# Way down of the experts: 128-column products in two column halves, or 256-column products in two contraction halves

## What is computed

```python
def expert_block(args):
    xblk, e = args
    hid = jax.nn.silu(xblk @ w_gate[e]) * (xblk @ w_up[e])   # 1024 -> 512
    return hid @ w_down[e]                                   # 512 -> 1024
```

## Time and profile before

| | |
|---|---|
| median of 3 runs | 4352.32 us |
| profiled execution | 4360.02 us, span 4358.2 us |
| TensorE (PE) busy | 3815.1 us, 88% of the span |
| VectorE (DVE) busy | 1654.0 us, 38% |
| ScalarE (ACT) busy | 941.3 us, 22% |
| mean granted clock of TensorE | 0.96 |
| the two expert stages' loops | about 605 and 599 us |

### The profile page before, as it was taken

One profiled execution on the slowest core, in us unless ns is written; L12 is line 12 of the kernel. 1 busy time (PEld: TensorE's weight loads), 2 busy tenths in 40 slices (PEclk: granted clock), 3 DMA queues, 4 the chain that ended last, 5 costly groups with the idle time before them and its releaser, 6 DMA issues.

```text
span 4358.2 us, 92432 instructions
## 1 busy us (share of the span) xinstructions
PE 3815.1 (88%) x35084; PEld 2225.2 (51%) x35085; DVE 1654.0 (38%) x3673; ACT 941.3 (22%) x2286; POOL 273.3 (6%) x453
## 2 busy tenths in 40 slices
PE   5997888999998889999889688888599997888884
PEld 3554665554444554444664355555344444555553
DVE  2576666413204661342562323222421124232225
ACT  3003544202002331230352211111110012111111
POOL 0000000000000000000000111111100001111111
PEclk9998999999999999999999899999799998999997
DMA  7111223101110000010331578999401114789994
GB/s 309 40 39 40 98 98 117 49 23 39 57 39 20 1 1 29 37 59 29 119 134 41 207 313 346 370 395 369 170 20 39 39 60 170 316 334 384 406 411 146
DMA packets 94338, 644.18 MB, mean 148 GB/s; under 512 B 18640, under 2 KB 41240, under 8 KB 60752
## 3 DMA queue, kind: packets, MB, share of 16 engines
q10 hardware_dynamic: 28896, 386.28, 21.1%
q1 hardware_dynamic: 46928, 194.98, 12.0%
q0 software_dynamic: 18336, 60.44, 4.1%
HBM read 594.70 MB, written 46.92 MB: 147 GB/s over the span
## 4 chain that ended last, share of the span: by engine, by line
PE 46%; issue 5%; DVE 4%; ACTq 3%; DMA 2%; ACT 1%; POOLq 0%; POOL 0%; DVEq 0%; SPq 0%
PE banks L258 22%; PE banks L2399 13%; PE banks L2408 4%; ACTq L2298 1%; PE banks L2394 1%; DMA arena<-y_tok,arena 1%; PE banks L1519 1%; PE banks L2390 1%; ACTq L2295 1%; DVE arena L1634 1%; PE banks L2120 1%; DMA arena<-in_w_gu 1%; ACTq L2292 1%; PE banks L467 1%; DMA h_tok<-arena 0%
## 5 line engine op out<-in xcount | busy, mean ns | idle before, releaser
L258 PE MATMUL banks<-arena 128*128 128x512 f32 (+2 forms) x4544 | 1749.7, 547 | 39.0 <-ACTq L137 16.9
L258 PEld LDWEIGHTS banks<-arena 128*128 128x128 f32 x4544 | 840.3, 191 | 936.4 <-issue 885.2
L2399 PE MATMUL banks<-arena 128*32 128x256 f32 x10240 | 637.1, 398 | 109.6 <-issue 104.3
L2399 PEld LDWEIGHTS banks<-arena 128*32 128x32 f32 x10240 | 333.6, 113 | 343.1 <-issue 178.7
L2408 PE MATMUL banks<-arena 128*32 128x128 f32 x10240 | 327.7, 275 | 55.3 <-DVE arena L2546 28.5
L2408 PEld LDWEIGHTS banks<-arena 128*32 128x32 f32 x10240 | 284.6, 110 | 105.5 <-issue 80.1
L1588 PE MATMUL banks<-arena 128*64 128x128 f32 x1952 | 162.1, 285 | 55.2 <-ACT arena L1601 39.5
L945 DVE SCALAR_TENSOR_TENSOR arena<-arena 128x1024 f32<-128x1024 f32 x240 | 195.9, 879 | 0.2 <-DVEq L137 0.2
L2365 POOL DMA_INDIRECT arena<-h_tok,arena x176 | 172.6, 981 | 142.2 <-POOL arena L2362 135.7
L301 DVE SCALAR_TENSOR_TENSOR arena<-banks,arena 128x512 f32<-128x512 f32 (+1 forms) x72 | 51.9, 721 | 333.5 <-PE banks L258 333.5
L1519 PE MATMUL banks<-arena 64*128 64x256 f32 (+2 forms) x768 | 129.7, 468 | 37.7 <-ACT arena L1690 32.8
(11 more groups left out here) (326 smaller groups left out, 3362.3 us busy)
## 6 DMA issues: line engine op xcount, KB each, us to landing
arena<-in_w_gu ACTq DMA_DIRECT2D x120, 2048.0 KB
arena<-in_w_dn ACTq DMA_DIRECT2D x60, 2048.0 KB
arena<-in_w_ada SPq DMA_DIRECT2D x24, 2048.0 KB, 7.3
y_tok<-arena SPq DMA_DIRECT2D x648, 32.0 KB
arena<-in_w_gu SPq DMA_DIRECT2D x8, 2048.0 KB
y_tok<-arena POOLq DMA_DIRECT2D x1, 12800.0 KB, 35.9
arena<-in_ab_w_ada SPq DMA_DIRECT2D x6, 2048.0 KB, 8.8
arena<-in_cd_w_ada SPq DMA_DIRECT2D x6, 2048.0 KB, 7.3
```

The lines of the kernel that those rows point to most:

```text
L258: last = pe.matmul(self.bank_of(g, n), lhsT, rhs, start=k == 0, stop=k == KT - 1)
L2399: last = pe.matmul(bank(2 + j)[32 * q:32 * q + 32, 0:256], xbT[:, 128 * j + 32 * q2:128 * j + 32 * q2 + 32], w_gu[slot][j][:, 4 * q2 + q], ...
```

## The change

The way down's two groups are no longer two column halves but two contraction halves, as on the way up. Group j takes contraction tiles 2j and 2j+1, writes all 256 columns of each strip in products of 256 columns, and has a bank of its own (6 or 7). A trip has 16 products (32 records of each kind) instead of 32 (64), each twice as wide. ScalarE copies the front group's bank 6 into a new buffer `y_part` (signal `yp`), and VectorE adds bank 7 to it and writes the sum to `y_sb` (signal `ya`). The addition for a block is issued in the next trip, behind the two copies into `hidS`; the last one of the stage stands behind the loops. The wait for room in `y_sb` moves from ScalarE to VectorE. TensorE waits for `h0` and `yp` before the front group and for `h1` and `ya` before the back group. Both inner loops of TensorE lose the branch hint.

```diff
-            def dn_half(self, pe, slot, h, chs):
-                for ch in chs:
+            def dn_half(self, pe, slot, j):
+                for ch in (2 * j, 2 * j + 1):
                     for q in range(4):
-                        last = pe.matmul(bank(6 + h)[32 * q:32 * q + 32, 0:128], hidS[:, 32 * ch:32 * ch + 32],
-                                         w_dn[slot][:, ch, 256 * q + 128 * h:256 * q + 128 * h + 128], start=ch == 0,
-                                         stop=ch == 3, tile_position=(0, 32 * q), skip_group_check=True)
+                        last = pe.matmul(bank(6 + j)[32 * q:32 * q + 32, 0:256], hidS[:, 32 * ch:32 * ch + 32],
+                                         w_dn[slot][:, ch, 256 * q:256 * q + 256], start=ch == 2 * j,
+                                         stop=ch == 2 * j + 1, tile_position=(0, 32 * q), skip_group_check=True)
...
-                    with self.trips(pe, begin, end) as b1:
-                        pe.wait_ge(self.y0, b1)
+                    with pe.Fori(begin, end) as b1:
                         pe.wait_ge(self.h0, b1)
-                        self.dn_half(pe, slot, 0, (0, 1))
+                        pe.wait_ge(self.yp, b1)
+                        self.dn_half(pe, slot, 0).then_inc(self.d0, 1)
                         pe.wait_ge(self.h1, b1)
-                        self.dn_half(pe, slot, 0, (2, 3)).then_inc(self.d0, 1)
-                        pe.wait_ge(self.y1, b1)
-                        self.dn_half(pe, slot, 1, (0, 1)).then_inc(self.dm, 1)
-                        self.dn_half(pe, slot, 1, (2, 3)).then_inc(self.d1, 1)
+                        pe.wait_ge(self.ya, b1)
+                        self.dn_half(pe, slot, 1).then_inc(self.d1, 1)
...
                 def down(i, slot, begin, end, nth=None):
                     with a.Fori(begin, end) as b1:
-                        room = a.snap((b1 & (XB - 1)) * 256)
-                        a.wait_ge(self.yf, b1)
+                        a.wait_ge(self.ya, b1)
                         a.sem_inc(passed, 1)
-                        a.wait_ge(self.d0, b1)
-                        a.activation(y_sb[:, bass.ds(room, 128)], bank(6)[:, 0:128], ACT.Copy).then_inc(self.y0, 1)
-                        a.wait_ge(self.d1, b1 + 1)
-                        a.activation(y_sb[:, bass.ds(room + 128, 128)], bank(7)[:, 0:128], ACT.Copy).then_inc(self.y1, 1)
+                        a.wait_ge(self.d0, b1 + 1)
+                        a.activation(y_part, bank(6)[:, 0:256], ACT.Copy).then_inc(self.yp, 1)
+                    a.wait_ge(self.d1, end)
+                    a.sem_inc(passed, 1)
...
+                def add_y(b1, room):
+                    d.wait_ge(self.yf, b1)
+                    d.wait_ge(self.yp, b1)
+                    d.tensor_tensor(y_sb[:, bass.ds(room, 256)], y_part, bank(7)[:, 0:256], ALU.add).then_inc(self.ya, 1)
...
                         at = d.snap(((b1 + 1) & (HELD - 1)) * 128)
-                        d.wait_ge(self.dm, b1)
+                        room = d.snap((b1 & (XB - 1)) * 256)
+                        d.wait_ge(self.d0, b1)
                         d.tensor_copy(hidS[:, 0:64], held[:, bass.ds(at, 64)]).then_inc(self.h0, 1)
                         d.wait_ge(self.d1, b1)
                         d.tensor_copy(hidS[:, 64:128], held[:, bass.ds(at + 64, 64)]).then_inc(self.h1, 1)
+                        add_y(b1, room)
```

More of the change, by code:

```diff
@@ L2053, in program @@
         gu_sum = mem(HT + 5248, 256)
+        y_part = mem(HT + 5504, 256)
         HELD = 64
@@ L2092, in __init__ @@
                 self.h0, self.h1 = s("hid_front"), s("hid_back")
-                self.d0, self.dm, self.d1 = s("down_0"), s("down_mid"), s("down_1")
-                self.y0, self.y1, self.yf = s("y_half_0"), s("y_half_1"), s("y_room")
+                self.d0, self.d1 = s("down_front"), s("down_back")
+                self.yp, self.ya, self.yf = s("y_part_kept"), s("y_added"), s("y_room")
                 self.yw = [s("y_stored_0"), s("y_stored_1")]
@@ L2325, in in_turn @@
                 return c0, c1
-            def trips(self, eng, begin, end):
-                return nc.Fori(begin, end, engines=bass.OrderedEngineSet([eng.engine]), hint_back_edge=True)
             def blocks_sp(self, sp):
@@ L2352, in blocks_sp @@
                             sp.dma_start(t["y_tok"][bass.ds((2 * m + i) * BLK, BLK), 256 * q:256 * q + 256],
-                                         y_sb[32 * q:32 * q + 32, bass.ds(((2 * m + i + 1) & (XB - 1)) * 256, 256)]
+                                         y_sb[32 * q:32 * q + 32, bass.ds(((2 * m + i + 2) & (XB - 1)) * 256, 256)]
                                          ).then_inc(self.yw[i], 16)
@@ L2459, in blocks_act @@
                 a.sem_inc(self.pc, 1)
-                a.sem_inc(self.y0, 1)
-                a.sem_inc(self.y1, 1)
+                a.sem_inc(self.yp, 1)
                 def silu(b1):
@@ L2495, in blocks_act @@
                 down(E - 1, 1, begin, top)
-                for half in (self.y0, self.y1):
-                    a.wait_ge(half, top)
-                    a.sem_inc(half, 1)
             def turned_half(self, d, j):
@@ L2508, in blocks_dve @@
             def blocks_dve(self, d):
-                d.sem_inc(self.yf, 6)
+                d.sem_inc(self.yf, 7)
                 d.sem_inc(self.g1, 1)
-                d.sem_inc(self.dm, 1)
+                d.sem_inc(self.d0, 1)
                 d.sem_inc(self.d1, 1)
@@ L2556, in blocks_dve @@
                 down(E - 1, 1, begin, top)
+                room = d.snap((top & (XB - 1)) * 256)
+                d.wait_ge(self.d1, top)
+                d.sem_inc(passed, 1)
+                add_y(top, room)
+                d.wait_ge(self.ya, top)
+                d.sem_inc(self.ya, 1)
             def sum_pool(self, g):
```

4 lines of the change are left out of this document (1 added, 3 removed).

## The result

The changed kernel takes 4301.94 us (median of 4 runs, 4291.37 to 4307.38); the kernel before 4349.39 us (4 runs, 4339.95 to 4359.52). The ratio is 0.9885, with an interval of 0.9867 to 0.9903: 47 us, or 1.1%, faster. The forecast was 22 us faster. The direction held and so did the range, by 2 us; the gain is more than twice the size.

The account below looks back on a forecast made before the run. The expert stages were taken to go at the pace of TensorE and its waits, weights close behind. Repeats 7.7, exits 8.4 and 6.4, less 0.3, gave 22 us: 4352.3 to 4330 us, range 4300 to 4378.

Parts of the forecast that it names:

- part 1: Way down's products: 32 records of 256 columns stream as long as 64 of 128, 1.73 us a trip; gain nothing.
- part 2: Way down's repeats: period from 2.18 to 2.09 us, closed by back copy and addition; 96 repeats gain 7.7 us.
- part 3: Exits to the next way up: 0.3 us at 28 with outer branch (8.4 us), 0.2 at 32 others (6.4 us).
- TensorE's clock is left out: Expert stages: half-clock stretches on TensorE not counted in the sum, moving the time by up to 10 us either way.
- part 5: TensorE's inner loops: branches take the same with or without hint, 221 against 222 ns; no cost inside loops.
- rival (c): Code layout or missing hint makes TensorE pause at exits or taken branches: 4361 or 4428 us; chance 0.04.
- part 4: VectorE: 68 us more additions, no cost at entries; y_sb wait nothing (bound +9.5); stage's last addition costs 0.3 us.
- part 6: Expert weight loads: DMA has 9.5 us to spare in the tightest stretch, which gains 4; nothing lost, bound 5 us.
- a sign of failure: TensorE's waits for expert weights (`in_w_gu`) over 10 us would show the forecast wrong.
- (a): TensorE arrives sooner but waits for ScalarE's silu or weights; only repeats pay, 4344 us; chance 0.36.
- (b): VectorE's addition bounds the way down's repeat, between `d1` and next back group: 2.4 us period, 4379 us; chance 0.12.
- (d): Weight loads and products were the bound, so the change only renames work: 4352 us; chance 0.02.

Follow-up runs that it names:

- run 1: Kernel after with both branch hints put back on TensorE's inner loops: 4319.53 us, 0.9929 of the kernel before.
- Run 7: Kernel after, contraction halves kept, but each strip's 256 columns made in two products of 128: 4322.37 us, 0.9943 of the kernel before.
- run 3: Kernel after with two more TensorE semaphore counts (0.19 us) at each exit with the outer branch: 4318.27 us, 0.9928 of the kernel before.
- run 4: Kernel before with filler, two unread 512-column products behind each way down of slot 1: 4324.11 us, 0.9945 of the kernel before.
- run 5: Kernel after with filler, two unread 512-column products behind each way down of slot 1: 4292.23 us, 0.9874 of the kernel before.
- run 6: Kernel before without branch hints and with the same two filler products: 4305.12 us, 0.9904 of the kernel before.
- run 9: Kernel after with ScalarE's reads of the next expert's number ahead of its waits for the products: 4271.84 us, 0.9815 of the kernel before.
- run 10: Kernel after with ScalarE's reads of the expert's number and of its next loop's bounds ahead of the waits: 4273.59 us, 0.9816 of the kernel before.
- run 8: Kernel after with VectorE's way-down addition done once more, into a spare buffer: 4313.39 us, 0.9913 of the kernel before.
- run 2: Kernel before with only its branch hints removed: 4325.93 us, 0.995 of the kernel before.

## Why the prediction was right and wrong

**Where the 47 us come from.** Over all executions the rest fell from 4180 to 4158 us and the clock's part from 169 to 142. So some 22 us are what the parts of the sum are about, and up to 27 are clock that the kernel before lost and the kernel after doesn't; with filler in both kernels the rest differs by 24. The medians of before (4349.4), with filler (4324.1), without hints (4305.1), with the new way down (4292.2), and that without filler (4301.9) make one path, 25 + 19 + 13 - 10, each step uncertain by some 8 us. But its inner steps aren't at an even clock: by the rest, the hints are 5 us and the new way down 19 on it. On the path without filler the rest gives 13 and 9. The two paths differ by the pause at the short exits, some 8 us in all (30 x 0.26), which is in the kernel before and in the one without hints and with filler, and in no other kernel of the two paths. With it taken out, the new way down is 9 to 11 us and the hints 5 to 13 (none by run 1); closer than that the runs don't divide the 22 us.

That the sum said 22 as well is in part luck. The sum has neither that pause, which the change removed, nor the 11.7 us more that TensorE waited for weights.

**The products (part 1).** Right. Run 7 has steady repeats of 2.08 to 2.12 us with 64 narrow records.

**The repeat's period (part 2).** Right: 2.09 forecast, 2.10 found, through the back copy and the addition. First repeats are as late as before (2.96 against 2.84 us, by ScalarE), 1.3 us more in all. The 52 later ones lost 17.7 us in all, more than forecast, since the second and third take 1.67 and 1.97. But the wait for the addition now stands inside a loop's last trip. Cut at each trip's first load, the 28 long exits became only 0.8 us shorter in all, though their idle fell by 7.4 (59.5 to 52.1), so about 7 us moved there. All trips together gained 17.7 - 1.3 - 7 = 9 us; the forecast was 7.7. One reading in it was incomplete: the pieces that it names for the old repeat add up to 2.07 us, and the sequencer's own 0.07 with 0.04 behind it make the 2.18. The new period doesn't rest on that.

**Exits (part 3).** Right in size. The idle of a long exit fell by 0.26 us, from a median of 2.12 to 1.86, where 0.3 was taken. At the short exits TensorE gained 0.65 us (3.16 to 2.51), of which some 0.25 is the pause, and gave about 0.4 back to the silu (12.9 us in all); net 0.2, as was taken, but with a pause in it that the forecast didn't have.

**The failed step** is the sentence "TensorE's clock is left out", with its "up to 10 us either way". The clock was no noise around the sum but followed from a term of it. The chain is: fewer records to hand out and no hint; 0.26 us less idle at the long exit; half clock behind 5 of 28 such exits instead of 20. Runs 3 and 4 show it from both sides: 0.19 us more idle brings stretches back and costs 16 us, work in the idle takes them away and gives 25. Seventeen stretches fewer at 1.6 us are 27 us in the two profiles, and over all executions the clock's part fell by the same 27; the sum had it at 0, with 10 at most. I had the row: the forecast read 0.95 and 0.96 in the stages, called it a few per cent and didn't ask where the low stretches stood. By those figures 8 to 10% of the 1204 us ran at half clock, and 605 x 0.05 + 599 x 0.04 = 54 us could be lost or won, five times the bound that was set. The stretches stood behind the very idle that part 3 shortened. The lower end of the range, 4300 us, held without a reason: the repeats' 7.7 us and exits of 0.6 us at 60 places give 4308, and 4304 at the exits' bound of 40 us, so the 4302 measured lies below what the named terms reach.

**The hint (part 5).** The second miss. The branch does cost the same within 14 ns (median 221 ns with hint; below, the loop of the way up in the kernel after, which has none), but the price is not in the branch.

```profile
L2423 PEldq COMPARE_BRANCH  x160: 67/207/219, 2477.1 to 4198.7; - x160
```

It is in the 0.09 us at the loop's head, which part 3 named and counted into its 0.3; in a pause that came with the layout of the kernel before; and in the clock. The Trainium skill, page "Runtime: NRT & Kernel Launch", section on instruction fetch mechanics, has a taken branch to a page outside the loaded ones wait for a fetch. That was rival (c), a pause at unhinted branches. The row above, of the way up's loop, speaks against it: none of its branches took over 219 ns, and none of the way down's. Pauses that move with the layout do exist here, and went the other way. That they are fetches no run shows.

**VectorE (part 4).** Right that an entry doesn't pay: entries are 4.9 us shorter in all, for which no run has the cause. The wait for room in `y_sb`, 9.5 us for ScalarE, costs the addition 0.4 us. **Weights (part 6):** waits went from 5.3 to 17.0 us, over the 10 that I had set as a sign of failure. The sign was badly chosen: a faster TensorE waits more for weights while the time falls.

**The rivals.** (a) was half true. ScalarE swallowed part of the gain: 12.9 us more idle before L2390, and the way up of runs 5 and 6, 10.6 us longer of which some 5 are clock; runs 9 and 10 show what it holds. (b) fell: the addition closes the repeat, but at 2.10 us, and twice the addition costs 11.5 us. Its price comes to 4379 us, where the range ends at 4378. (c) fell, and its opposite came. (d) fell.

**What stays open.** At the same idle of 1.86 us, 1, 5, 5 and 6 of 28 long exits were followed by half clock (run 9, the kernel after, runs 10 and 8). So the length decides how often, not whether, and what decides the rest wasn't tried. What makes the pause of 0.25 us move wasn't tried either.

## What to carry to other kernels

Look up where the low stretches of the granted clock stand before an edit is costed: an idle gap of TensorE that recurs in front of long work has a price beyond its own length, here 1.6 us for each gap that was followed by half clock, and a few tenths off it, or unused products in it, pay several times over. When TensorE is made to arrive sooner, ask which small steps of another engine (here ScalarE's register reads behind a wait) come last there, and move those ahead of the wait. Compare variants at an even clock before a gain is put down to an edit: filler in all of them brings the clocks closer, and span x granted clock, taken over every execution and not only the profiled one, shows how much is left between them.

## What was unexpected in the hardware

- **Half clock after about 2 us of idle.** Medians of the idle at the long exits, and behind how many of the 28 half clock began within 6 us: 2.12 us, 20 (before); 2.05, 12 (run 3); 2.02, 13 (run 1); 2.01 and 2.02, 14 and 16 (runs 7 and 2); 1.86, 5 (after). The products ahead of these exits had been running at 2.4 GHz.
- **Adding work made the kernel faster:** 128 records of filler, 64 us busy, took 25 us off the kernel before and 5 (by the ratios) to 10 (by the medians) off the kernel after.
- **A hint costs without being waited for:** 0.09 us at the head of each loop, and nothing back at the branch (median 221 ns with it against 207).
- **Pauses of the sequencer that come and go with the code's place:** the median short exit of the kernel before is 3.16 us as it is, 2.90 with filler, 2.79 without hints, 3.06 with neither hints nor idle at the other exit. That is up to 0.27 us, 30 times, without any change to the work at that place.
